# Scaling a gated layer's values by thirds, and moving the norms' second sums behind the next weight split

## The chip, the cores and the metric
The kernel runs on one core of one Trainium2 chip. The metric is the device time of one execution in microseconds (us), as the median of several runs. A profiled execution gives the trace from which every duration below is read. TensorE (PE), VectorE (DVE), ScalarE (ACT), GpSimd (POOL) and SyncE (SP) each run their own instruction stream and wait for each other on semaphores.

## What is computed
The input x has 512 positions of 1024 values. Three layers follow one another, each with a normalisation that is modulated from a conditioning vector c:

```
mod = silu(c) @ ada_w + ada_b                     # shifts, scales, gates
h   = rms_norm(x) * (1 + sc1) + sh1
y   = chunked_relpos_attention(h)                 # layer 0
y   = chunked_spatial_gating(h)                   # layer 1, the gated layer
x   = x + g1 * y
h   = rms_norm(x) * (1 + sc2) + sh2
x   = x + g2 * (relu(h @ w1)**2 @ w2)             # feed-forward of layers 0 and 1
x   = hybrid_layer(x)                             # layer 2: sparse attention and a state space part
```

The gated layer is

```
z    = gelu(h @ w_in);  u, v = split(z)           # 3072 columns each
v    = rms_norm(v)
vm   = W_s v + b_s                                # mixes positions inside windows of 128
y    = (u * vm) @ w_out
```

All arithmetic is 32-bit. A matrix product is computed as three products of a high and a low part.

## The kernel before
**Weights.** All weights pass through SBUF as 136 slabs of 128x2048 numbers. SyncE loads a slab into one of two raw buffers as soon as the slab two before it has been split. A slab is split in two steps: ScalarE copies it to its high part (`w_hi`, line 1050), VectorE subtracts to get the low part (`w_lo`, line 1480). There are two buffers for the parts too, so ScalarE's copy of a slab waits until TensorE is through with the slab two before (`slab_used`), and TensorE waits for `lo_done` before its first product with a slab. Line 474 holds the three products of every step.

**Order.** Nothing schedules the work: each engine's instructions stand in the order in which the code of its block issues them, and an instruction that waits holds back all that stand behind it on its engine. Results go to eight PSUM banks used in turn; `bank()` on TensorE waits (`acc_free`) until the bank used eight turns ago has been released.

**Tails and heads.** The last product of each of the first four blocks (attention out, feed-forward 0, gated layer out, feed-forward 1) is a `tail`, and what follows is a `head`. In a tail the last four of eight output tiles are computed in two halves of 256 positions: `half_tiles(x, 0)`, then `half_tiles(x, 1)`, over the same two slabs. While TensorE does the second half, ScalarE and VectorE already normalise the first. For each half the norm goes: ScalarE squares the tiles (`square`, line 1105), VectorE adds them up (`add_square`, line 1537), TensorE sums over the partitions with a vector of ones (`sums`, lines 533 and 534), ScalarE takes the root (`root`, line 1136), VectorE inverts it (`invert`, line 1584), TensorE spreads it (`spread`, line 543), and then `apply` on VectorE and `high_norm` on ScalarE make the high and low parts of h (lines 1597, 1149, 1606). The head's first products need h of the first half (`h_ready`) and its first slab; those with the second half of h come after two slabs' worth of half tiles. In `head` (before a feed-forward) the second half's `sums(1)` stands after the first half tile, `(j, m, k) == (0, 0, 7)`, and `spread(1)` six steps later, at `(0, 1, 5)`. In `head_natural` (before the gated and the hybrid layer) they stand after the first and the second tile of slab 0, and both result banks of a half are taken before its first product.

In what follows the two slabs of a head are called C and D, and the slab after them E. ScalarE splits C in the middle of `high_norm(0, split)`. It splits D in its `head()`, after the four squares of the second half. VectorE does its part of C in `apply(0, split)` and of D at the start of its `head()`, ahead of `invert(1)`. E is split at tile 6 of `ffn` (`if o == 6`), on ScalarE and VectorE.

**Modulation.** GpSimd loads the 128x1024 pieces of `ada` into two buffers in turn, and VectorE multiplies each with c and sums it (`ada`, line 1504). `ADA_FFN` says at which slabs of a quarter of a feed-forward VectorE takes one piece; the eight slots of a quarter are its four up slabs (0 to 3) and its four down slabs (4 to 7). Beside the slabs VectorE also does stages of tables for the state space part (`s5_stage`), and GpSimd stores these tables; the order of its loads and stores is derived from `ADA_FFN` too.

**Gated layer.** After the six panels of v, VectorE reduces the squares, inverts the root and scales v by position (line 2024: four instructions, one for each 128 positions, all 3072 columns). Then come three chunks of eight tiles of u: TensorE multiplies a tile of u (24 products), then mixes the same tile of v in `mix` (line 809); the first mix waits for `bv_scaled`.

```
for t in range(TT):
    ts_(b_v[:, t, :], b_v[:, t, :], rstd[:, t:t + 1], None, ALU.mult).then_inc(sem("bv_scaled"), 1)
for ch in range(CHUNKS):
    for s in range(4):
        split()
```

## Time and profile before
| | |
|---|---|
| median of 3 runs | 1845.28 us (1842.94 to 1848.31) |
| the profiled execution | 1844.67 us, of which the trace's span is 1842.5 us |
| TensorE busy | 1760.9 us, 96% of the span |
| VectorE busy | 1165.5 us, 63% |
| ScalarE busy | 667.8 us, 36% |
| GpSimd busy | 101.3 us, 5% |
| granted TensorE clock, mean | 0.99 |
| DMA | 245.98 MB, mean 134 GB/s |

The busy shares are averages over stages of different kinds, so what a change is worth is read at its place: in the timeline (what an engine did when, and in brackets how long it had been idle and who released it), in the table of waits (who waited for whom, in total), in the chain of waits (followed back from the end) and in the windows (busy time and granted clock in a stretch).

### The profile page before, as it was taken

How to read it: one execution, taken by the hardware profiler on the slowest of the kernel's cores; microseconds unless marked ns; L12 is line 12 of the kernel's file. 1: busy time of each engine (PE TensorE's matmuls, PEld its weight loads, DVE VectorE, ACT ScalarE, POOL GpSimd, SP SyncE). 2: the span in 40 equal slices, each digit the busy share in tenths (PEclk: the TensorE clock that was granted, in tenths of full speed). 3: DMA queues.
4: the chain of work that ended last, by engine and by line, in shares of the span. 5: the costliest groups of instructions: out<-in, count | busy, mean ns of one | idle time of the engine just before them, and what ended most of it. 6: DMA issues, size and time to landing. Idle time of an engine off the chain costs nothing.

```text
span 1842.5 us, 24232 instructions
## 1 busy us (share of the span) xinstructions
PE 1760.9 (96%) x9361; PEld 1465.6 (80%) x9361; DVE 1165.5 (63%) x2373; ACT 667.8 (36%) x1081; POOL 101.3 (5%) x194
## 2 busy tenths in 40 slices
PE   3998999999999999999999999999999998999999
PEld 2776768888888888878888898888888987777787
DVE  6777766876467656564454548874676579445574
ACT  3423673423232333233232335322323332366432
POOL 0001100001000100100000000010001100000000
PEclk9999999999999999999999999999999999999999
DMA  9354324335333534642323224354336222300351
GB/s 367 115 181 162 115 69 145 138 114 186 120 115 136 172 114 155 212 164 92 137 91 138 75 97 146 135 171 164 140 129 201 96 91 92 127 34 24 138 195 46
DMA packets 45470, 245.98 MB, mean 134 GB/s; under 512 B 6256, under 2 KB 6480, under 8 KB 27440
## 3 DMA queue, kind: packets, MB, share of 16 engines
q1 hardware_dynamic: 24848, 155.36, 23.3%
q0 software_dynamic: 20512, 89.11, 14.4%
q8 instruction: 74, 1.21, 0.3%
q14 instruction: 36, 0.29, 0.1%
HBM read 229.23 MB, written 15.22 MB: 133 GB/s over the span
## 4 chain that ended last, share of the span: by engine, by line
PE 81%; DVE 11%; ACT 3%; issue 2%; DMA 2%; SPq 0%; DVEq 0%; ACTq 0%
PE ps L474 70%; DVE w_lo L1480 2%; PE ps L935 2%; DMA ada_raw<-in_ada 1%; PE ps L809 1%; PE ps L916 1%; PE ps L925 1%; ACT w_hi L1050 1%; PE ps L644 1%; DVE ada_raw L1504 1%; PE ps L667 1%; PE ps L653 1%; DVE ada_first L1865 1%; DVE pre L1597 1%; PE ps L957 1%
## 5 line engine op out<-in xcount | busy, mean ns | idle before, releaser
L1480 DVE TENSOR_TENSOR w_lo<-w_raw,w_hi 128x2048 fp32r<-128x2048 f32 x136 | 311.6, 2291 | 153.8 <-ACT w_hi L1050 153.5
L1050 ACT ACTIVATE w_hi<-w_raw 128x2048 fp32r<-128x2048 f32 x136 | 260.0, 1912 | 361.7 <-PE ps L474 339.0
L474 PE MATMUL ps<-h_hi,w_hi 128*128 128x512 f32 (+1 forms) x1008 | 379.1, 376 | 9.9 <-DVE w_lo L1480 6.5
L474 PE MATMUL ps<-h_lo,w_hi 128*128 128x512 f32 (+1 forms) x1008 | 374.8, 372 | 0.0
L474 PE MATMUL ps<-h_hi,w_lo 128*128 128x512 f32 (+1 forms) x1008 | 374.5, 372 | 0.0
L474 PEld LDWEIGHTS ps<-h_hi,w_hi 128*128 128x128 f32 x1008 | 191.8, 190 | 43.7 <-DVE w_lo L1480 7.0
L474 PEld LDWEIGHTS ps<-h_hi,w_lo 128*128 128x128 f32 x1008 | 191.7, 190 | 32.6
L474 PEld LDWEIGHTS ps<-h_lo,w_hi 128*128 128x128 f32 x1008 | 191.8, 190 | 31.3
L474 PE MATMUL ps<-hid_hi,w_hi 128*128 128x512 f32 (+1 forms) x576 | 211.3, 367 | 0.0
L474 PE MATMUL ps<-hid_hi,w_lo 128*128 128x512 f32 (+1 forms) x576 | 210.6, 366 | 0.0
L474 PE MATMUL ps<-hid_lo,w_hi 128*128 128x512 f32 (+1 forms) x576 | 210.5, 366 | 0.0
L474 PE MATMUL ps<-w_hi,h_hi 128*128 128x512 f32 (+1 forms) x480 | 187.1, 390 | 17.4 <-DVE h_lo L1885 9.9
L474 PE MATMUL ps<-w_lo,h_hi 128*128 128x512 f32 (+1 forms) x480 | 184.2, 384 | 0.0
L474 PE MATMUL ps<-w_hi,h_lo 128*128 128x512 f32 (+1 forms) x480 | 183.8, 383 | 0.0
L1504 DVE CUSTOM_DVE_ANT_0 ada_raw<-ada_raw,cond 128x1024 f32<-128x1024 f32 x104 | 126.0, 1221 | 45.2 <-DMA ada_raw<-in_ada 44.1
L474 PEld LDWEIGHTS ps<-w_hi,h_hi 128*128 128x128 f32 x480 | 93.2, 194 | 38.3 <-issue 6.3
L474 PEld LDWEIGHTS ps<-hid_hi,w_hi 128*128 128x128 f32 x576 | 108.6, 189 | 17.7
L474 PEld LDWEIGHTS ps<-hid_lo,w_hi 128*128 128x128 f32 x576 | 108.6, 189 | 17.6
L474 PEld LDWEIGHTS ps<-hid_hi,w_lo 128*128 128x128 f32 x576 | 108.6, 189 | 17.3
L395 POOL DMA_DIRECT2D ada_raw<-in_ada x104 | 55.6, 535 | 1049.3 <-DVE mod_s L1504 985.2
L474 PEld LDWEIGHTS ps<-w_hi,h_lo 128*128 128x128 f32 x480 | 93.2, 194 | 17.1
L474 PEld LDWEIGHTS ps<-w_lo,h_hi 128*128 128x128 f32 x480 | 93.2, 194 | 16.5
(395 smaller groups left out, 2400.5 us busy)
## 6 DMA issues: line engine op xcount, KB each, us to landing
w_raw<-in_slabs SPq DMA_DIRECT2D x136, 1024.0 KB, 4.8
ada_raw<-in_ada POOLq DMA_DIRECT2D x104, 512.0 KB, 5.1
s_tables<-s_tab POOLq DMA_DIRECT2D x4, 2692.0 KB, 9.2
s_t<-s_tables POOLq DMA_DIRECT2D x4, 2692.0 KB, 9.8
ada_first<-in_ada SPq DMA_DIRECT2D x16, 512.0 KB, 15.1
a_bias<-in_a_bias POOLq DMA_DIRECT2D x16, 256.0 KB, 3.3
xT<-in_xT SPq DMA_DIRECT2D x4, 512.0 KB, 6.3
s_toeplitz<-KTp POOLq DMA_DIRECT2D x32, 64.0 KB, 3.3
```

The lines of the kernel that those rows point to most:

```text
L395: gp.dma_start(ada_raw[:, k % 2, :], I["ada"][k]).then_inc(sem(f"ada_in{k % 2}"), 16)
L474: last = mm(o, l, r, start=start and n == 0, stop=stop and n == 2)
L644: last = mm(ps[(s + j) % 3][:, 0:n], q, k, start=True, stop=True)
L653: last = nc.tensor.transpose(ps[3 + u % 2][:, j:j + P], a_p[:, u % 8, j:j + P], ident[:])
L667: last = mm(ps[5 + i % 2][HD * par:HD * par + HD, it * P:(it + 1) * P], value(UNITS_A[u + par], j), a_pt[:, (u + par) % 4, j * P:(j + 1) * ...
L809: last = mm(b[:, t * P:(t + 1) * P], b_v[:, t, gm * P:(gm + 1) * P], b_ws[:, gm // 3, :], start=True, stop=True)
L916: last = mm(ps[(s + g) % 3][:, 0:n], hqr[r, i, ts], hk[r, br - 1, 0:n], start=True, stop=True)
L925: last = nc.tensor.transpose(ps[3 + u % 2][:, j:j + P], h_p[:, u % 5, j:j + P], ident[:])
L935: last = mm(o, h_pt[:, u % 3, j * P:(j + 1) * P], hv[:, j, vc], start=j == 0, stop=j == it)
L1050: A(w_hi[s][:], w_raw[:, s, :], ACT.Copy).then_inc(sem("hi_done"), 1)
L1480: tt(w_lo[s][:], w_raw[:, s, :], w_hi[s][:].bitcast(F32), ALU.subtract).then_inc(sem("lo_done"), 1)
L1504: V.tensor_tensor_reduce(out=w, in0=w, in1=cond[:, which, :], scale=1.0, scalar=0.0, op0=ALU.mult, op1=ALU.add, accum_out=mod_s[:, o:o + 1 ...
```

## The change
Four things change. The values of the gated layer are scaled for the first 1024 columns only before the chunks, and each later third in four instructions, one after each split of the four u slabs of the chunk before (`scale_v`). `ADA_FFN` of layer 0 has slot 1 in place of slot 0. ScalarE splits D right behind `high_norm(0, split)`, ahead of the squares of the second half. TensorE does `sums(1)` and `spread(1)` later: in `head` at `(0, 1, 5)` and `(1, 0, 3)`, in `head_natural` after the second tile of slab 0 and after the first tile of slab 1; and there each bank is taken just before its first product.

```diff
--- before.py
+++ after.py
@@ -49,7 +49,7 @@
 ADA_FIRST = 16
 
 ADA_QKV = 16
-ADA_FFN = (4, (0, 2, 4, 5)), (6, (0, 1, 2, 3, 4, 5))
+ADA_FFN = (4, (1, 2, 4, 5)), (6, (0, 1, 2, 3, 4, 5))
 ADA_BV = 0, 4, 4, 5, 4, 4
 
 
@@ -588,9 +588,9 @@
             def head():
 
                 def beside(j, m, k):
-                    if (j, m, k) == (0, 0, KT - 1):
+                    if (j, m, k) == (0, 1, 5):
                         sums(1)
-                    if (j, m, k) == (0, 1, 5):
+                    if (j, m, k) == (1, 0, 3):
                         spread(1)
                 reserve(1)
                 half_tiles(H, 0, lambda k: h_ready(0, k), beside)
@@ -601,11 +601,13 @@
 
                 reserve(1)
                 for half in range(2):
-                    bs = [bank(), bank()]
+                    bs = []
                     for j in range(2):
                         s = (c.base("slab") + j) % 2
                         wait(pe, "lo_done", c("slab", 1 + j))
                         for t in range(2):
+                            if j == 0:
+                                bs.append(bank())
                             ts = slice(HT * half + t * P, HT * half + (t + 1) * P)
                             for kk in range(4):
                                 k, cols = 4 * j + kk, slice(kk * 512, (kk + 1) * 512)
@@ -616,11 +618,10 @@
                                 last.then_inc(sem("slab_used"), 1)
                             elif j:
                                 last.then_inc(sem("acc_full"), 1)
-                            if half == 0 and j == 0:
-                                if t == 0:
-                                    sums(1)
-                                if t == 1:
-                                    spread(1)
+                            if (half, j, t) == (0, 0, 1):
+                                sums(1)
+                            if (half, j, t) == (0, 1, 0):
+                                spread(1)
                 c.add("slab", 2)
                 c.add("norms")
 
@@ -802,8 +803,8 @@
                     def mix(m):
 
                         gm = KT * ch + 2 * s + m
-                        if gm == 0:
-                            pe.wait_ge(sem("bv_scaled"), TT)
+                        if gm % KT == 0:
+                            pe.wait_ge(sem("bv_scaled"), TT * (ch + 1))
                         b = bank()
                         for t in range(TT):
                             last = mm(b[:, t * P:(t + 1) * P], b_v[:, t, gm * P:(gm + 1) * P], b_ws[:, gm // 3, :], start=True, stop=True)
@@ -1123,6 +1124,7 @@
                     square(o, 0)
                 root(0)
                 high_norm(0, split)
+                split()
                 for o in range(4, KT):
                     c.add("bank")
                     c.add("slab" if o % 2 else "full")
@@ -1152,7 +1154,6 @@
 
             def head():
 
-                split()
                 root(1)
                 high_norm(1)
 
@@ -2020,11 +2021,18 @@
             V.tensor_reduce(stat[:, 0:TT], vss[:], AX.X, ALU.add).then_inc(sem("v_red"), 1)
             dve.wait_ge(sem("v_std"), 1)
             step(V.reciprocal(rstd[:, 0:TT], stat[:, 0:TT]))
+
+            def scale_v(t, ch):
+                v = b_v[:, t, KT * P * ch:KT * P * (ch + 1)]
+                ts_(v, v, rstd[:, t:t + 1], None, ALU.mult).then_inc(sem("bv_scaled"), 1)
+
             for t in range(TT):
-                ts_(b_v[:, t, :], b_v[:, t, :], rstd[:, t:t + 1], None, ALU.mult).then_inc(sem("bv_scaled"), 1)
+                scale_v(t, 0)
             for ch in range(CHUNKS):
                 for s in range(4):
                     split()
+                    if ch < CHUNKS - 1:
+                        scale_v(s, ch + 1)
                     for m in range(2):
                         gm = KT * ch + 2 * s + m
                         full(m)
```

**ScalarE at the end of a tail** (here the attention's; the four tails read alike). `w_hi` and `w_hi_54` are the two high buffers, C and D in this order; `pre`, `h_hi` belong to the norm, `sq_x`, `sq_84` are the squares, `stat` is the root. Before:

```order
L1149 ACTIVATE h_hi<-pre_87,mod 128x256 x4
L1050 ACTIVATE w_hi<-w_raw 128x2048
L1149 ACTIVATE h_hi<-pre_87,mod 128x256 x4
L1105 ACTIVATE sq_x<-xT 128x256 x3
L1105 ACTIVATE sq_84<-xT 128x256
L1050 ACTIVATE w_hi_54<-w_raw 128x2048
L1136 ACTIVATE stat<-ps,eps 128x2
```

and now:

```order
L1151 ACTIVATE h_hi<-pre_87,mod 128x256 x4
L1051 ACTIVATE w_hi<-w_raw 128x2048
L1151 ACTIVATE h_hi<-pre_87,mod 128x256 x4
L1051 ACTIVATE w_hi_54<-w_raw 128x2048
L1106 ACTIVATE sq_x<-xT 128x256 x3
L1106 ACTIVATE sq_84<-xT 128x256
L1138 ACTIVATE stat<-ps,eps 128x2
```

D's split moved from behind the four squares to ahead of them.

**VectorE at the start of the gated layer's chunks.** `b_v` are the values, `b_vm` the mixed tile, `g_lo` the low part of the product. Before:

```order
L2022 RECIPROCAL rstd<-stat 128x4
L2024 TENSOR_SCALAR b_v<-b_v,rstd 128x3072 x4
L1480 TENSOR_TENSOR w_lo_56<-w_raw,w_hi_54 128x2048
L2037 SCALAR_TENSOR_TENSOR b_vm<-ps,bv_g,b_bs 128x512
L2041 TENSOR_TENSOR b_vm<-b_vm,b_u 128x512
L2043 TENSOR_TENSOR g_lo<-b_vm,g_hi 128x512
L2037 SCALAR_TENSOR_TENSOR b_vm<-ps,bv_g,b_bs 128x512
L2041 TENSOR_TENSOR b_vm<-b_vm,b_u 128x512
```

and now:

```order
L2023 RECIPROCAL rstd<-stat 128x4
L2027 TENSOR_SCALAR b_v<-b_v,rstd 128x1024 x4
L1481 TENSOR_TENSOR w_lo_56<-w_raw,w_hi_54 128x2048
L2027 TENSOR_SCALAR b_v<-b_v,rstd 128x1024
L2045 SCALAR_TENSOR_TENSOR b_vm<-ps,bv_g,b_bs 128x512
L2049 TENSOR_TENSOR b_vm<-b_vm,b_u 128x512
L2051 TENSOR_TENSOR g_lo<-b_vm,g_hi 128x512
L2045 SCALAR_TENSOR_TENSOR b_vm<-ps,bv_g,b_bs 128x512
```

The four instructions became a third as wide, and one more of this width stands behind each split of the first two chunks.

**VectorE in the first quarter of the first feed-forward**, around tiles 4 and 5 and the split of E (`w_lo`); the two `ISA` rows are one piece of the modulation. Before:

```order
L1733 SCALAR_TENSOR_TENSOR s_t_176<-s_kk,s_th 128x8
L1734 SCALAR_TENSOR_TENSOR s_th<-s_kk,s_t_176 128x8
L1735 TENSOR_SCALAR s_th<-s_th 128x8
L1504 ISA ada_raw,mod_s<-ada_raw,cond 128x1024
L1504 ISA mod_s 128x1
L1666 SCALAR_TENSOR_TENSOR relu_94<-ps,relu 128x256
L1698 TENSOR_TENSOR hid_lo<-relu_94,hid_hi 128x256
L1666 SCALAR_TENSOR_TENSOR relu_94<-ps,relu 128x256
L1698 TENSOR_TENSOR hid_lo<-relu_94,hid_hi 128x256
L1480 TENSOR_TENSOR w_lo<-w_raw,w_hi 128x2048
```

and now:

```order
L1734 SCALAR_TENSOR_TENSOR s_t_176<-s_kk,s_th 128x8
L1735 SCALAR_TENSOR_TENSOR s_th<-s_kk,s_t_176 128x8
L1736 TENSOR_SCALAR s_th<-s_th 128x8
L1667 SCALAR_TENSOR_TENSOR relu_94<-ps,relu 128x256
L1699 TENSOR_TENSOR hid_lo<-relu_94,hid_hi 128x256
L1667 SCALAR_TENSOR_TENSOR relu_94<-ps,relu 128x256
L1699 TENSOR_TENSOR hid_lo<-relu_94,hid_hi 128x256
L1481 TENSOR_TENSOR w_lo<-w_raw,w_hi 128x2048
```

The piece that stood ahead of tile 4 (`relu_94`) now stands behind E's split and the table stage that follows it.

## Rows read from the trace of the kernel before

**Rows 1.** The page, part 1: busy time, share of the span, instructions, by engine.
```profile
PE 1760.9 (96%) x9361; PEld 1465.6 (80%) x9361; DVE 1165.5 (63%) x2373; ACT 667.8 (36%) x1081; POOL 101.3 (5%) x194
```

**Rows 2.** Waits of TensorE over the whole run: us in total, times, longest.
```profile
PE ps L809 <- DVE b_v L2024: 4.1, 1, 4.1
PE ps L533 <- ACT sq L1105: 4.0, 2, 2.0
PE ps L474 <- DVE pre L1597: 3.7, 2, 1.8
```

**Rows 3.** Timeline of VectorE where the values are scaled: start us, us, instruction, idle before.
```profile
820.46 7.01 DVE L2024 TENSOR_SCALAR b_v<-b_v,rstd 128x3072 f32<-128x3072 f32 x4
```

**Rows 4.** Chain of waits, same place: start us, us, what.
```profile
827.52 1.85 PE ps L809 x8
829.37 6.39 PE ps L474 x24
836.65 5.46 PE ps L474 x24
```

**Rows 5.** Windows: us, busy PE, PEld, DVE, ACT, POOL, granted clock, DMA, GB/s.
```profile
827.50:829.40 1.90, 1.88 (x9) 1.88 (x10) 1.90 (x1) 0.00 (x0) 0.00 (x0) 0.58 0.00 0
342.37:345.27 2.90, 0.01 (x2) 0.01 (x1) 2.35 (x2) 2.87 (x9) 0.00 (x0) 1.00 0.40 160
682.31:684.14 1.83, 0.00 (x1) 0.03 (x1) 1.83 (x6) 0.84 (x2) 1.53 (x3) 1.00 0.14 54
684.14:688.55 4.41, 4.41 (x13) 3.47 (x13) 3.48 (x10) 2.53 (x6) 0.55 (x2) 0.61 0.96 364
```

**Rows 6.** VectorE by form: a scaling 512 wide.
```profile
L1978 DVE TENSOR_SCALAR a_p<-a_p,row_inv 128x512 f32<-128x512 f32 x16 | 7.1, 484 | 0.3
```

**Rows 7.** Head of the first feed-forward, timelines of ScalarE, VectorE and TensorE.
```profile
315.31 0.51 ACT L1149 ACTIVATE h_hi<-pre,mod 128x256 fp32r<-128x256 f32 x1 [0.28 <-DVE pre L1597]
316.89 0.81 ACT L1105 ACTIVATE sq_x<-xT 128x256 f32<-128x256 f32 x2 [1.07 <-DVE xT L1542]
319.25 1.90 ACT L1050 ACTIVATE w_hi<-w_raw 128x2048 fp32r<-128x2048 f32 x1
...
318.81 0.41 DVE L1537 TENSOR_TENSOR acc<-acc,sq_x 128x256 f32<-128x256 f32 x1
321.25 2.29 DVE L1480 TENSOR_TENSOR w_lo<-w_raw,w_hi 128x2048 fp32r<-128x2048 f32 x1 [2.02 <-ACT w_hi L1050]
...
319.40 0.38 PE L533 MATMUL ps<-ones,acc 128*128 128x1 f32 x2 [1.98 <-ACT sq L1105]
...
323.67 0.71 PE L543 MATMUL ps<-ident,rstd 128*128 128x128 f32 x4 [0.97 <-DVE rstd L1584]
```

**Rows 8.** Chain of waits, between the first half's two norm products.
```profile
304.64 2.25 PE ps L474 x18
```

**Rows 9.** Same feed-forward, where its third slab is split: VectorE, then ScalarE.
```profile
337.45 0.17 DVE L1735 TENSOR_SCALAR s_th<-s_th 128x8 f32<-128x8 f32 x1
339.06 1.22 DVE L1504 CUSTOM_DVE_ANT_0 ada_raw<-ada_raw,cond 128x1024 f32<-128x1024 f32 x1 [1.44 <-DMA ada_raw<-in_ada]
...
340.99 1.90 ACT L1050 ACTIVATE w_hi<-w_raw 128x2048 fp32r<-128x2048 f32 x1
```

**Rows 10.** Head of the gated layer, timelines of VectorE, ScalarE and TensorE.
```profile
680.30 2.29 DVE L1480 TENSOR_TENSOR w_lo<-w_raw,w_hi 128x2048 fp32r<-128x2048 f32 x1 [0.41 <-ACT w_hi L1050]
...
683.30 0.47 DVE L1597 SCALAR_TENSOR_TENSOR pre<-xT,mod_a,ps 128x256 f32<-128x256 f32 x1
...
687.74 1.90 ACT L1050 ACTIVATE w_hi<-w_raw 128x2048 fp32r<-128x2048 f32 x1
...
692.21 0.60 PE L543 MATMUL ps<-ident,rstd 128*128 128x128 f32 x4
```

**Rows 11.** Second feed-forward, its third slab: VectorE's split, TensorE's first product.
```profile
1135.78 2.29 DVE L1480 TENSOR_TENSOR w_lo<-w_raw,w_hi 128x2048 fp32r<-128x2048 f32 x1 [1.07 <-ACT w_hi L1050]
...
1138.35 0.40 PE L474 MATMUL ps<-h_hi,w_hi 128*128 128x512 f32 x1
```

## The prediction

> **What bounds the kernel now.** I read the page first, then TensorE's waits, then the places where they stand. The page shows TensorE busy for 1760.9 of 1842.5 us [rows 1], so the most that any reordering can return is 81.6 us of idle time, and what an edit returns has to be found in a wait of TensorE that it shortens. In the table of waits the reader is to see three that the diff touches [rows 2]: one of 4.1 us for the scaled values, two of 2.0 us for the squares ahead of `sums(1)`, two of 1.8 us for the last `pre` of a first half. The chain of waits then shows what follows the first of them, and the windows show the granted clock behind such waits. All times below are those of one profiled execution of 1844.67 us (span 1842.5, 2.2 around it); the median of the runs is 0.6 above it. About 0.3%, or 5.5 us, is what a measurement can tell from no change here.
>
> **The scaling.** Four instructions of 3072 columns take 7.01 us from 820.46 [rows 3]. TensorE wanted the values 4.1 us before 827.52, at 823.4. Behind the wait it is slow as well: the mix and the next tile took 1.85 and 6.39 us where the later pair takes 0.89 (835.76 to 836.65) and 5.46 [rows 4]; the granted clock is 0.58 there, so most of that stretch ran at the lower of the two levels, 1.2 instead of 2.4 GHz [rows 5]. From 823.4 to 836.65 are 13.2 us; undisturbed the same work (mix, tile, mix) is 0.89 + 5.46 + 0.89 = 7.2. So the wait costs 6.0 us in all. Now: 512 columns take 0.48 us [rows 6], 3072 take 1.75, so 1024 take 0.48 + (1.75 - 0.48) / 5 = 0.74 and four of them 3.0: ready at 823.4, as TensorE comes. What is left of the wait lies between 0 and 0.2 us, and a wait of that size was followed by a low clock nowhere; I take 0. **Term: -6.0.** The other eight instructions (5.9 us of VectorE) go beside u slabs of 2 x 6.35 us on TensorE, in which no wait for VectorE stands now; nothing shows. If that cover went, each would cost 0.74. The mixes of the later thirds find their values ready over 20 us early.
>
> **The piece of modulation in the first feed-forward.** Ahead of E's split VectorE ends its table stage at 337.6, waits 1.44 us for a load, works on the piece, and only at 340.2 takes up tile 4; ScalarE's part of E follows at 340.99 [rows 9], and TensorE stands from 342.37 to 345.27 [rows 5]. Without the piece this chain is 340.2 - 337.6 = 2.6 us shorter and E can start at 342.7. **Term: -2.6**, if nothing earlier in the head moves VectorE. The piece itself (1.2 us, its load long landed) comes after the split, beside E's 48 products of 0.23 us, 10.9 in all [rows 4]. In later quarters it changes slots beside slabs of 11 us; GpSimd's load for slot 4 now stands behind the eight table stores, two slabs or 22 us before its use. Nothing for these.
>
> **The heads before the two feed-forwards.** ScalarE now does D's split at the end of the high parts, 315.8, to 317.7; the first square, at 316.89 before, comes 0.8 later [rows 7]. From it to `sums(1)` were 2.5 us, so the sums can go at 320.2. TensorE was there at 317.4 and waited 1.98; now it has 18 products more to do, which take 2.25 [rows 8], so it comes at 319.7 and waits 0.5. D's low part starts behind the last add (319.2 + 0.8 = 320.0) and is there at 322.3, where it was 323.5. The sums take 1.0 (319.40 to 322.70, where TensorE stood before the spread, less the 2.25), six products 0.7: TensorE is at D at 321.9, waits 0.5, does twelve more, 1.4, and spreads at 323.8, where it was 323.67. So the second half's norm comes no earlier, but TensorE stands 18 products further on: 2.1 us gained. Its steps with the second half's h then begin at about 328.6, at 0.36 each, while VectorE finishes them every 0.8 us until about 331; by this the last one is just in time (0 to 0.5 us lost). But E holds the gain back. In the first feed-forward TensorE comes to E at 340.3 and waits until 342.7, so the term above is all. In the second no slot moved: E's low part was there at 1138.07 and TensorE started at 1138.35 without waiting [rows 11]; now it comes at 1136.2 and waits about 2 us. **Term: -0.2**, between -0.4 and 0.
>
> **The heads before the gated and the hybrid layer.** TensorE was free at 682.31, C's low part there at 682.6, but the first tile started at 684.14 [rows 5, 10], since the second of its two banks is released by the last `pre`, which ends at 683.8. Now the first tile needs one bank less and starts at 682.8. Its two tiles end at 688.3. This head follows the first one at 368.5 us (D's split at 687.74 against 319.25 [rows 7, 10]), so its sums can go at 320.2 + 368.5 = 688.7, end at 689.7, and D is there at 690.9: a wait of 1.2. Half a slab, 2.73, then the spread, 0.6, and another 2.73: the second half starts at 696.9. Before it was 692.21 + 0.6 + 5.46 = 698.3. The low clock behind the 1.83 us wait cost nothing then, because the spread had to wait for D (687.74 + 1.90 + 2.29 = 691.9) and the inversion behind it anyway. **Term: 2 x -1.4 = -2.8.**
>
> **Sum** with the clock as it was: -6.0 - 2.6 - 0.2 - 2.8 = -11.6, 1833.1 us.
>
> **The clock.** A stretch at the low level costs 4.41 x (1 - 0.61) = 1.7 us [rows 5]. Behind waits of 1.83 us (two) and 2.90 us it came, behind the two of 2.0 it did not [rows 2, 7]: three of five. After the change three such places stand where nothing absorbs it: the wait for E in the second feed-forward (2.0 us, new), and in the two natural heads a row of 0.5, 0.4 and 1.2 us with the tiny products of the sums between. I count one and a half of three, the broken ones being the less likely: 2.6 us. So -11.6 + 2.6 = -9.0, 1835.7 on this execution and up to 1836.3 on the median; I forecast 1835.9.
>
> The Trainium skill (TensorE: Matmul & The Clock Gate, Part 1) puts the low level behind TensorE standing idle throughout; by that rule none of the three places would slow down, and the time would be 1833.1. The rows speak against it, since 1.83 us of idling was enough twice. The same section says that the monitor runs free, so that one kernel differs from run to run; no run here shows that yet.
>
> **Rivals.**
> - *No low clock at the three places.* What the page's rule would give. For it: the two 2.0 us waits, the broken waits. Against it: the 1.83 us ones. 1844.7 - 11.6 = 1833.1.
> - *Waits that only move.* All three places slow down, 5.1 us, and TensorE catches up with the second half's h in each head, up to 0.5 each: -11.6 + 5.1 + 0 to 2 = -6.5 to -4.5, 1838 to 1840. For it: VectorE's norm is no earlier than before while TensorE is. Against it: the steps' arithmetic above comes out just in time.
> - *D's split becomes the bound; slower.* On ScalarE the four squares now stand behind an instruction that waits for D's raw slab and for the end of the tail. If it waits x us beyond 315.8, the squares, the sums, D's low part and the spread are x late, and TensorE, which already waits at the sums and at D, loses x in each of four heads. From x = 2.3 the gain is gone, from 3.6 the kernel is over 0.3% slower; at x = 4 it is 1835.7 + 16 = 1852. For it: the order leaves no other work to ScalarE there. Against it: TensorE is through with the tail before ScalarE gets there (in the first head it began the first half tile, 24 products or 2.9 us, before 317.4, so by 314.5; in the gated one it was free at 682.31, where ScalarE will be ready at 315.8 + 368.5 = 684.3), and D's load is issued when the slab two before it is split.
> - *The change doesn't do what it says*: the thirds could be late, with a mix of a later chunk waiting. They are issued a whole chunk ahead, so I give it nothing of its own.
>
> **How the numbers follow.** Forecast, one or two places slow, 1834 to 1838: 0.54. No low clock: 0.20. Waits that only move: 0.21, a third of it still under 1839.7. Slower: 0.05. Faster by over 0.3% then is 0.54 + 0.20 + 0.07, about 0.80; within 0.3% 0.15; slower 0.05. The range goes from no low clock, less 0.7 for runs that scatter, to the far end of the second rival: 1832.4 to 1840.4.
>
> **What would show it.** In the changed kernel: the wait for `b_v` at line 809's mix gone or under 0.2 us, and no low clock in that chunk; the first feed-forward's wait for E still over 2 us but ending 2.6 earlier relative to C; a new wait of about 2 us for E in the second; both `pre` waits gone and a wait for D's low part of about 1.2 in the natural heads; the squares' wait at 0.5. Wrong would be: D's split on ScalarE waiting for a semaphore, waits for h in the second half's steps, the clock low behind each head, or VectorE late for a slab in the first two chunks.

## The result and the profile after

| | before | changed |
|---|---|---|
| median of the runs | 1845.28 us (1842.94 to 1849.24, 5 runs) | 1832.71 us (1830.98 to 1836.74, 5 runs) |
| the profiled execution, its span | 1844.67 us, 1842.5 us | 1832.71 us, 1830.5 us |
| TensorE busy | 1760.9 us | 1757.2 us |

The ratio of the two is 0.9927, with an interval from 0.9914 to 0.994: 0.7% faster, some 12.6 us by the medians and 12.0 us by the profiled executions. (The ratio is not the quotient of the two medians, which is 0.9932; 0.9927 stands for 13.5 us.) Forecast were 9.0 us on the profiled execution, and 1835.9 us in a range of 1832.4 to 1840.4. The median lies just inside the lower end of that range; the ratio applied to the median of before gives 1831.8, which is outside. The direction and the list of places came out; the gain is larger than forecast.

The page of the changed kernel, part 1, answers to [rows 1]:

```profile
PE 1757.2 (96%) x9361; PEld 1462.1 (80%) x9361; DVE 1166.0 (64%) x2381; ACT 666.9 (36%) x1081; POOL 101.2 (6%) x194
```

TensorE's busy time fell by 3.7 us though it does the same 9361 products. That part of the gain is the clock, since products at the low level count as busy for longer (the 12 products further down take 4.45 us at a granted clock of 0.62 and 2.87 at 1.00). The other 8.3 us of the span are waits that are gone. TensorE's waits, as in [rows 2]:

```profile
PE ps L474 <- DVE w_lo L1481: 14.1, 9, 3.6
...
PE ps L474 <- issue: 2.0, 4, 0.5
...
PE ps L533 <- ACT sq L1106: 1.0, 2, 0.6
```

The waits for `b_v` (4.1) and for `pre` (3.7) are in the table no more, and the one for the squares fell from 4.0 to 1.0 us. The spreads' waits for `rstd` in the two feed-forwards, one of them in [rows 7], are gone too. In their place the waits for a low part grew. These are the two rows of before:

```profile
PE ps L474 <- DVE w_lo L1480: 10.2, 4, 3.6
...
PE ps L543 <- DVE rstd L1584: 2.3, 2, 1.3
```

Gone are 4.1 + 3.7 + 3.0 + 2.3 = 13.1 us. What came are 3.9 us for low parts and two starts of a head at which TensorE waits 0.5 us on its own issue, where before it waited for `pre`: 4.9 us, 8.2 net, close to the 8.3 above. The rows of the table that the change doesn't touch moved too, one by as much as 1.5 us, but they nearly cancel (0.3 us less together).

**The scaling.** Timeline of VectorE at the start of the gated layer's chunks, against [rows 3]:

```profile
814.91 2.74 DVE L2027 TENSOR_SCALAR b_v<-b_v,rstd 128x1024 f32<-128x1024 f32 x4
817.57 2.28 DVE L1481 TENSOR_TENSOR w_lo<-w_raw,w_hi 128x2048 fp32r<-128x2048 f32 x1
819.77 0.75 DVE L2027 TENSOR_SCALAR b_v<-b_v,rstd 128x1024 f32<-128x1024 f32 x1
820.43 0.74 DVE L2045 SCALAR_TENSOR_TENSOR b_vm<-ps,bv_g,b_bs 128x512 f32<-128x512 f32 x1
```

Four scalings 1024 wide take 2.74 us where the forecast had 3.0. They end at 817.65, and the first mix begins at 817.70. TensorE is busy for the whole 15 us around it, at the high level:

```profile
817.70 1.16 PE L810 MATMUL ps<-b_ws,b_v 128*128 128x128 f32 x8
```

```profile
811.00:826.00 15.00, 15.00 (x76) 12.53 (x75) 9.72 (x17) 7.10 (x8) 0.00 (x0) 1.00 0.22 77
```

The last scaling of the second third ends at 857.69, and the first mix that needs it starts at 912.10, so no later chunk is near a wait.

**The head of the first feed-forward**, TensorE, against [rows 7]:

```profile
314.62 0.36 PE L474 MATMUL ps<-h_hi,w_hi 128*128 128x256 f32 x1 [0.50 <-issue]
...
320.32 0.38 PE L533 MATMUL ps<-ones,acc 128*128 128x1 f32 x2 [0.45 <-ACT sq L1106]
...
322.40 0.38 PE L474 MATMUL ps<-h_hi,w_hi 128*128 128x256 f32 x1 [0.21 <-DVE w_lo L1481]
...
323.93 0.60 PE L543 MATMUL ps<-ident,rstd 128*128 128x128 f32 x4
...
342.79 0.50 PE L474 MATMUL ps<-h_hi,w_hi 128*128 128x512 f32 x1 [2.41 <-DVE w_lo L1481]
```

The forecast had the sums at 320.2, D at 322.4 (wait 0.5), the spread at 323.8 and E at 342.7. (This kernel reaches the tail 0.3 us later, at 303.99 against 303.69; counted from there, all four came 0.2 to 0.3 us earlier than forecast.) ScalarE in the same place:

```profile
315.62 0.51 ACT L1151 ACTIVATE h_hi<-pre,mod 128x256 fp32r<-128x256 f32 x1 [0.27 <-DVE pre L1598]
316.04 1.90 ACT L1051 ACTIVATE w_hi<-w_raw 128x2048 fp32r<-128x2048 f32 x1
```

D's split follows the last high part at once and waits for nothing.

**The head of the gated layer**, TensorE, against [rows 5, 10]:

```profile
678.71 0.47 PE L474 MATMUL ps<-w_hi,h_hi 128*128 128x512 f32 x1 [0.50 <-issue]
...
684.42 0.38 PE L533 MATMUL ps<-ones,acc 128*128 128x1 f32 x2
...
686.50 0.50 PE L474 MATMUL ps<-w_hi,h_hi 128*128 128x512 f32 x1 [1.03 <-DVE w_lo L1481]
...
689.37 0.61 PE L543 MATMUL ps<-ident,rstd 128*128 128x128 f32 x4
```

The head starts 0.50 us after the tail, no longer 1.83, and the wait for D's low part is 1.03 us. To compare the two kernels, count from the tail's first-half sums (672.19 before, 668.08 now): the second half's products began at 25.94 and begin at 24.49, 1.45 us earlier.

**The second feed-forward, and the head of the hybrid layer**, TensorE:

```profile
1126.54 0.50 PE L474 MATMUL ps<-h_hi,w_hi 128*128 128x512 f32 x1 [1.78 <-DVE w_lo L1481]
```

```profile
1470.26 0.50 PE L474 MATMUL ps<-w_hi,h_hi 128*128 128x512 f32 x1 [1.03 <-DVE w_lo L1481]
...
1474.71 0.60 PE L543 MATMUL ps<-ident,rstd 128*128 128x128 f32 x4
```

There is the new wait for E, 1.78 us where 2.0 was forecast. In the hybrid head the stretch from D to the spread takes 4.45 us, in the gated head 2.87 for the same 12 products. The windows give the reason (the granted clock is the third number from the end):

```profile
342.79:346.79 4.00, 4.00 (x18) 3.31 (x19) 3.66 (x24) 0.86 (x4) 0.53 (x1) 1.00 0.71 248
686.50:689.37 2.87, 2.87 (x12) 2.36 (x13) 0.03 (x1) 0.00 (x0) 0.00 (x0) 1.00 1.01 373
1126.54:1130.54 4.00, 4.00 (x18) 3.31 (x19) 3.67 (x24) 0.87 (x4) 0.53 (x1) 1.00 0.68 248
1470.26:1474.71 4.45, 4.45 (x13) 3.51 (x13) 0.02 (x1) 0.00 (x0) 0.00 (x0) 0.62 0.65 236
```

Of four places where TensorE starts again behind a wait, one is at the low level. In the kernel before, the stretch behind the wait for E was low too. This is its window (not among the rows above):

```profile
345.27:349.27 4.00, 4.00 (x12) 3.20 (x13) 3.10 (x23) 2.02 (x4) 0.00 (x0) 0.66 0.71 242
```

**Where the 12 us came from.** The program falls into five pieces, cut at the first-half sums of the four tails (line 533; before at 303.69, 672.19, 1099.47 and 1463.54, now at 303.99, 668.08, 1088.03 and 1451.84):

| piece | before | now | gain | of it |
|---|---|---|---|---|
| up to tail 1 | 303.69 | 303.99 | -0.3 | nothing of the change |
| first feed-forward | 368.50 | 364.09 | 4.4 | E 2.8 earlier; 1.6 clock behind E |
| gated layer | 427.28 | 419.95 | 7.3 | head 1.45; scaling 5.9 |
| second feed-forward | 364.07 | 363.81 | 0.3 | E as good as kept its place |
| hybrid layer | 378.96 | 378.66 | 0.3 | head 1.45, less 1.6 clock; 0.4 unexplained |

### The profile page after: what moved, and what is told of

Read it like the earlier page. It is cut to its first block, busy times and chain, and to the rows that moved or that the text cites. A ratio compares the mean times of both kernels' runs of the same rounds, so it can differ in the third digit from the quotient of the medians.

```text
span 1830.5 us, 24238 instructions
## 1 busy us (share of the span) xinstructions
PE 1757.2 (96%) x9361; PEld 1462.1 (80%) x9361; DVE 1166.0 (64%) x2381; ACT 666.9 (36%) x1081; POOL 101.2 (6%) x194
## 4 chain that ended last, share of the span: by engine, by line
PE 80%; DVE 12%; ACT 4%; issue 2%; DMA 2%; SPq 0%; DVEq 0%; ACTq 0%
PE ps L474 69%; DVE w_lo L1481 3%; PE ps L936 2%; PE ps L810 1%; DMA ada_raw<-in_ada 1%; PE ps L917 1%; ACT w_hi L1051 1%; DVE ada_raw L1505 1%; PE ps L926 1%; DVE ada_first L1866 1%; PE ps L645 1%; DVE pre L1598 1%; PE ps L654 1%; PE ps L668 1%; PE ps L958 1%
```

## The experiments

The theory under test is the forecast's own. Each edit returns the wait of TensorE that it takes away, unless something else is late at the same place; and behind each wait that is left, a low clock may or may not follow. Its rivals are that a wait only moves to the next engine that is late, that the clock and not the waits made the gain, and that one edit alone carries it. Each expectation, quoted as it was written, states what its theories give. All ratios are against the kernel before, run beside it on the same chip (medians 1846.52, 1846.14 and 1846.24 us in three groups of runs).

### The parts one at a time

**The thirds alone.**

```diff
-    ts_(b_v[:, t, :], b_v[:, t, :], rstd[:, t:t + 1], None, ALU.mult).then_inc(sem("bv_scaled"), 1)
+    scale_v(t, 0)
...
+        if ch < CHUNKS - 1:
+            scale_v(s, ch + 1)
```

> The kernel before with the scaling by thirds alone. Theory A (the terms add, each at its own place): the wait of 4.1 us for the values and the low clock behind it go, 5.9 us off, ratio 0.9968. Rival B (the low clock is a matter of chance and comes elsewhere): only the wait itself goes, 4.1 us, ratio 0.9978, and a low stretch stands in the gated chunks as before. Both: no wait of a chunk's mix for b_v, the four heads with the waits of before (2.0 at the sums, 1.8 before the natural heads, 2.9 for E).

Measured: 1837.74 us, ratio 0.9967 [0.995, 0.9984]. The gated piece took 421.40 us (672.87 to 1094.27), against 427.28: 5.88 us, the whole term. The waits in the heads stood as before, the 2.93 us one for E among them, but for one: the squares before the hybrid layer, for which TensorE now waits 0.76 us.

**Slot 1 in place of slot 0 alone.**

```diff
-ADA_FFN = (4, (0, 2, 4, 5)), (6, (0, 1, 2, 3, 4, 5))
+ADA_FFN = (4, (1, 2, 4, 5)), (6, (0, 1, 2, 3, 4, 5))
```

> The kernel before with slot 1 for slot 0 in layer 0 alone. Theory A: E of the first feed-forward starts 2.6 us earlier while TensorE comes to it as before (342.37), so the wait falls from 2.9 to 0.3 and the low clock behind it goes too: 2.6 + 1.7 = 4.3 us off, ratio 0.9977. Rival B (the waiting in the head decides, not the slot): under 1 us off, a wait for E of over 2 us left. Both: nothing at the other three heads.

Measured: 1841.43 us, ratio 0.9984 [0.9968, 1.0]. TensorE at E, in the kernel with the slot alone:

```profile
341.73 0.50 PE L474 MATMUL ps<-h_hi,w_hi 128*128 128x512 f32 x1 [0.25 <-DVE w_lo L1480]
```

The wait shrank from 2.90 to 0.25 us, and the piece of the program took 364.23 us, against 368.50: 2.65 us of wait and 1.6 of clock, since here the wait of 0.25 us was not followed by a low level. The profiled execution, 1849.69 us in all, had a long stretch of low clock in the hybrid layer, which the change doesn't touch; the total of this trace says nothing, its first piece does.

**Everything in the heads alone** (sums, spreads, D's split, banks; the scaling and the slot as before).

```diff
+                split()                       # ScalarE, behind high_norm(0, split)
-                    if (j, m, k) == (0, 0, KT - 1):
+                    if (j, m, k) == (0, 1, 5):
                         sums(1)
...
-                    bs = [bank(), bank()]
+                    bs = []
```

> The kernel before with D's split moved, the sums and spreads later and the banks taken one by one, without thirds and slot. Theory A: E of the first feed-forward still starts at about 345.2 with a wait of over 4.5 us (the gain there moves into the wait), 0.2 off in the second feed-forward, 1.4 in each natural head less 1.7 for each low clock: 1 to 3 us off, ratio 0.9984 to 0.9995. Rival C (the heads are what made the change better than forecast): 5 us or more off, ratio under 0.9973.

Measured: 1844.43 us, ratio 0.9991 [0.9982, 1.0001]. In the first feed-forward the head passes TensorE on earlier and E takes all of it back:

```profile
346.04 0.57 PE L474 MATMUL ps<-h_hi,w_hi 128*128 128x512 f32 x1 [4.62 <-DVE w_lo L1481]
```

4.62 us of wait for E, where 2.90 stood, and the low level behind it. This is the forecast's sentence "E holds the gain back", shown. (E itself starts 42.54 us behind the tail's sums, 41.58 before: in this trace a low level at 322.44 to 325.85, behind waits of 0.43 and 0.21 us in the head, came before it; without one, in the run of sums and split below, E starts at 41.44.) In the gated head D's products took 2.86 us, in the hybrid one 4.44:

```profile
691.38:694.24 2.86, 2.86 (x12) 2.36 (x13) 0.02 (x1) 0.00 (x0) 0.00 (x0) 1.00 1.01 375
1482.23:1486.67 4.44, 4.44 (x13) 3.49 (x14) 0.02 (x1) 0.00 (x0) 0.00 (x0) 0.62 0.69 236
```

**The banks alone.**

```diff
-                    bs = [bank(), bank()]
+                    bs = []
...
+                            if j == 0:
+                                bs.append(bank())
```

> The kernel before with the banks of the natural heads taken one by one, nothing else. Theory A: the first tile starts 1.4 us earlier, but the sums then wait for the squares (about 2.4 us) and the spread for D as before: 0 us off, ratio 0.9995 to 1.0005, with a wait at line 533 in place of the one for pre. Rival D (the bank alone gives the 1.5 us of each natural head): 3 us off, ratio 0.9984.

Measured: 1848.31 us, ratio 1.0014 [1.0005, 1.0023], slower by a little. The head of the gated layer, TensorE:

```profile
681.38 0.47 PE L474 MATMUL ps<-w_hi,h_hi 128*128 128x512 f32 x1 [0.50 <-issue]
...
686.47 0.38 PE L533 MATMUL ps<-ones,acc 128*128 128x1 f32 x2 [2.08 <-ACT sq L1107]
...
690.67 0.71 PE L543 MATMUL ps<-ident,rstd 128*128 128x128 f32 x4 [0.30 <-DVE rstd L1586]
```

The head begins 1.3 us earlier and the sums then wait 2.08 us for the squares: the wait moved. I hadn't expected a loss. The gated piece is as long as before (427.09 against 427.28 us). In the hybrid head the spread comes 21.04 us behind the tail's sums, 20.02 before: the stretch of low clock now lies behind the sums, close ahead of the spread, where nothing is left to absorb it. In the gated head of this trace the clock stayed high, and the spread comes at 19.91. That is 1.0 us in one head of one trace; the rest of the 2.6 us that the ratio says is not placed.

### The parts taken out one at a time

**The changed kernel again**, for its scatter.

> The changed kernel once more. Theory A (low clocks fall by chance at waits of about 2 us, each costing up to 1.7 us): the waits stand where they stood in the changed kernel, to 0.1 us (0.5 and 0.2 in the first head, 2.4 for E, 1.0 for D in the natural heads, 1.8 for E in the second feed-forward), but the low stretches stand at other places; ratio 0.992 to 0.995. Rival B (which wait slows the clock is fixed by the kernel): a low stretch at the hybrid layer's head alone, as in the changed kernel's trace.

Measured: 1834.05 us (1833.28 to 1834.14, 5 runs), ratio 0.9937 [0.9924, 0.9951]. Its waits in the heads and for E are those of the first trace, to 0.03 us. The clock is not. This is the window behind E:

```profile
341.27:345.27 4.00, 4.00 (x12) 3.21 (x13) 3.66 (x24) 0.87 (x4) 0.53 (x1) 0.64 0.67 231
```

The same wait of 2.41 us was followed by 0.64 here and by 1.00 in the trace above. The first feed-forward took 365.45 us, against 364.09.

**Without the thirds.** The edit is the first diff of this section, undone on the changed kernel.

> The changed kernel with all 3072 columns scaled at once, as before the change. Theory A: the wait of 4.1 us at the first mix and its low clock are back, 5.9 us more than the changed kernel, so heads, banks and slot together give 5 to 7 us, ratio 0.996 to 0.9975, which is more than slot alone (0.9984) and heads alone (0.9991) and near their sum (0.9975). Rival E (the parts multiply each other): under 0.995.

Measured: 1838.99 us, ratio 0.9963 [0.9951, 0.9975]. The wait of 4.11 us for `b_v` is back, and so is the low level behind it:

```profile
824.25:826.15 1.90, 1.90 (x9) 1.90 (x10) 1.90 (x1) 0.00 (x0) 0.00 (x0) 0.56 0.00 0
```

**Sums and split without the banks**, and nothing else of the change. The diff is against the kernel with everything in the heads.

```diff
-                    bs = []
+                    bs = [bank(), bank()]
...
-                            if j == 0:
-                                bs.append(bank())
```

> The kernel before with D's split and the sums moved, but both banks of a natural head taken at once as before. Theory A: the first tile of a natural head starts behind a wait of 1.8 us as before, then no wait for the sums, D ready: if the clock falls behind that wait the second half starts as late as before (0 us off in that head), if not 1.3 us off; so this is 0 to 3 us slower than with the banks (0.9991), ratio 0.9990 to 1.0005. Rival F (the banks give nothing in this company either): the same ratio as with them, 0.9991.

Measured: 1844.03 us, ratio 0.9993 [0.9984, 1.0002], against 0.9991 with the banks. The two waits of 1.83 us for `pre` are back at the start of the natural heads. The gated head, TensorE:

```profile
683.56 0.47 PE L474 MATMUL ps<-w_hi,h_hi 128*128 128x512 f32 x1 [1.83 <-DVE pre L1596]
...
689.11 0.28 PE L533 MATMUL ps<-ones,acc 128*128 128x1 f32 x2
...
692.88 0.61 PE L543 MATMUL ps<-ident,rstd 128*128 128x128 f32 x4
```

The head starts 1.3 us later than with the banks and then waits for nothing, neither squares nor D. Its spread stands 21.27 us behind the tail's sums; in the changed kernel it is 21.29. D's low part ends at 689.97 and TensorE takes it up at 690.02, 18.41 us behind the tail's sums; in the changed kernel, after its wait of 1.03 us, it is 18.42. So it is D's low part that sets the spread, and where TensorE spends its wait ahead of that, before C or before D, is all one. The banks are worth nothing measurable (the gated piece took 425.82 us, and 425.80 with them), and the 1.45 us of this head belong to the sums and the split.

**The sums and spreads where they were**, the rest of the change in (the edit in `head`; the one in `head_natural` is alike).

```diff
-                    if (j, m, k) == (0, 1, 5):
+                    if (j, m, k) == (0, 0, KT - 1):
                         sums(1)
-                    if (j, m, k) == (1, 0, 3):
+                    if (j, m, k) == (0, 1, 5):
                         spread(1)
```

> The changed kernel with sums(1) and spread(1) where they were before. Theory A: the squares come 0.8 us later and the sums are asked for at the old place, so TensorE waits 2.8 us in the two heads of feed-forwards and some 3.2 us in the natural heads, where its spread then also waits or nearly does; 1.5 us lost in each natural head and a low clock more likely there: 4 to 8 us slower than the changed kernel, ratio 0.995 to 0.9975. Rival G (the place of the sums does not matter since D's low part sets the pace): within 1.5 us of the changed kernel, ratio 0.9925 to 0.9940.

Measured: 1840.07 us, ratio 0.9966 [0.9954, 0.9979]. ScalarE's split ahead of the squares makes them late, and TensorE, which has not been given other work, stands for it in all four heads, 2.60 to 2.74 us. The gated one, and the clock behind it, which was low in all four heads:

```profile
685.47 0.59 PE L533 MATMUL ps<-ones,acc 128*128 128x1 f32 x2 [2.71 <-ACT sq L1107]
```

```profile
685.47:689.47 4.00, 4.00 (x13) 3.52 (x14) 2.20 (x2) 0.26 (x1) 0.00 (x0) 0.50 1.02 357
```

**D's split where it was**, the rest of the change in.

```diff
-                high_norm(0, split)
-                split()
+                high_norm(0, split)
...
             def head():
+                split()
                 root(1)
```

> The changed kernel with ScalarE splitting D behind the squares, as before. Theory A (D's low part sets the pace of the head): no wait for the squares, but D's low part comes 1.2 us later, TensorE waits for it about 2 us before the feed-forwards and 2.3 before the gated and hybrid layer, and each head ends 1.1 to 1.3 us later: 4.8 us slower than the changed kernel, a low clock more likely, ratio 0.996 to 0.998. Rival H (moving the sums alone does the work, D's split is free): ratio 0.9925 to 0.9940, the same as the changed kernel.

Measured: 1842.51 us, ratio 0.9987 [0.9974, 1.0]. The sums no longer wait, but D's low part is late and TensorE stands at D in all four heads. The gated one:

```profile
690.35 0.50 PE L474 MATMUL ps<-w_hi,h_hi 128*128 128x512 f32 x1 [2.74 <-DVE w_lo L1481]
```

In the first head the spread starts 22.63 us behind the tail's sums, 19.94 in the changed kernel, and E 41.55, against 38.80. So 2.7 us of lateness in the head go on to E and take the slot's term with them. Of these, 1.5 us are D itself (its first product is at 19.91 us, against 18.42); the rest is the clock, which was low in this head from 323.02 to 326.43, and in the other three too. The expectation had 4.8 us of loss against the changed kernel and a ratio of 0.996 to 0.998; the medians say 8.5 to 9.8 us, the four pieces behind the first tail 9.1. D was 1.3 to 1.5 us late where 1.1 to 1.3 was expected, and the low level, which came in every head, had been called "more likely" and given no price. The sums without the split lose, and the split without the sums loses; the two moves are one edit.

### Beyond the change

**The same slot move in the second feed-forward**, on top of the change. There too a piece of modulation stands ahead of E's split, and E's wait of 1.78 us is new.

```diff
-ADA_FFN = (4, (1, 2, 4, 5)), (6, (0, 1, 2, 3, 4, 5))
+ADA_FFN = (4, (1, 2, 4, 5)), (6, (1, 2, 3, 4, 5, 6))
```

> The changed kernel with layer 1's pieces at slots 1 to 6 instead of 0 to 5. Theory A (E's wait in the second feed-forward is VectorE's chain ahead of its split): the piece of 1.2 us leaves that chain, the wait of 1.8 us falls to 0.6, 1.2 us off the changed kernel and no low clock behind it. Rival B (the chain there is bound by ScalarE or by the release of C): the wait stays at 1.8, nothing changes. Ratio to the kernel before 0.992 to 0.9935.

Measured: 1830.81 us (1828.63 to 1834.30, 4 runs), ratio 0.9909 [0.9895, 0.9923].

```profile
1128.14 0.50 PE L474 MATMUL ps<-h_hi,w_hi 128*128 128x512 f32 x1 [0.67 <-DVE w_lo L1481]
```

E starts 37.39 us behind the tail's sums, 38.51 in the changed kernel, and the piece of the program takes 362.70 us, against 363.81: 1.1 us gained, all of it at E. It has the lowest median of all kernels here. It is faster than the kernel before, and by more than was expected (0.992 to 0.9935). Against the changed kernel its interval overlaps that one's first, 0.9914 to 0.994, and just misses its second, 0.9924 to 0.9951; what speaks for the edit is the 1.1 us of the trace, which is the size that the theory gave.

**Two more pieces of modulation behind E's split** in the first feed-forward.

```diff
                             if o == 4:
...
-                                if layer == 0:
-                                    ada(2, 0)
-                                    ada_put()
                                 beside(0)
                             if o == 6:
                                 split()
+                                if layer == 0:
+                                    ada(2, 0)
+                                    ada_put()
```

> The changed kernel with the two pieces and the put that stand ahead of tile 4 in the first feed-forward moved behind E's split. Theory A: VectorE's chain to E is 2.5 us shorter, the wait of 2.4 us for E becomes 0 to 0.2, 2.3 us off the changed kernel and no low clock at this place in any run. Rival B (the two pieces only use time that VectorE has): the wait stays over 2 us. Ratio to the kernel before 0.991 to 0.993.

Measured: 1836.95 us (1832.38 to 1847.04, 8 runs), ratio 0.995 [0.9934, 0.9967]. The medians are 2.9 and 4.2 us above those of the changed kernel's two groups, but the interval overlaps both of theirs. The gain that the theory forecast did not come. E's wait did shrink, to 0.46 us, but against the changed kernel E is only 0.4 us earlier (38.37 us behind the tail's sums, against 38.80), and TensorE arrives 1.5 us later. That lateness is not the edit's: in this trace, and in the next one, a low level stood in the head, behind the waits of 0.43 and 0.21 us:

```profile
322.42:326.42 4.00, 4.00 (x23) 4.00 (x22) 0.93 (x3) 0.41 (x1) 0.00 (x0) 0.57 0.73 264
```

The kernel without the thirds has the same code here, without this edit, and its trace has the same low stretch: there E came at 39.91, behind a wait of 2.00 us. So at a like clock the edit makes E 1.5 us earlier. That is less than the 2.5 us expected of the chain, in part because VectorE now waits 0.79 us there for ScalarE's share of the table stage. What it costs comes one slab later, as TensorE and VectorE tell (F is the slab after E):

```profile
341.95 0.50 PE L474 MATMUL ps<-h_hi,w_hi 128*128 128x512 f32 x1 [0.46 <-DVE w_lo L1481]
...
355.12 0.50 PE L474 MATMUL ps<-h_hi,w_hi 128*128 128x512 f32 x1 [1.99 <-DVE w_lo L1481]
```

```profile
341.81 1.22 DVE L1505 CUSTOM_DVE_ANT_0 ada_raw<-ada_raw,cond 128x1024 f32<-128x1024 f32 x1
...
342.96 1.22 DVE L1505 CUSTOM_DVE_ANT_0 ada_raw<-ada_raw,cond 128x1024 f32<-128x1024 f32 x1
...
348.92 1.23 DVE L1505 CUSTOM_DVE_ANT_0 ada_raw<-ada_raw,cond 128x1024 f32<-128x1024 f32 x1 [2.59 <-DMA ada_raw<-in_ada]
...
352.78 2.29 DVE L1481 TENSOR_TENSOR w_lo<-w_raw,w_hi 128x2048 fp32r<-128x2048 f32 x1 [1.06 <-ACT w_hi L1051]
```

```profile
343.33 0.55 POOL L395 DMA_DIRECT2D ada_raw<-in_ada  x1 [28.30 <-DVE mod_s L1505]
```

Three pieces now stand in a row with two buffers between them. GpSimd can issue the third load only when the first piece is done, at 343.33, and VectorE, which may not pass it by, waits 2.59 us until 348.92. Behind it stand the next tile and F's split. F comes 1.99 us late, where no wait was, and a low clock follows. The piece of the program took 367.60 us, against 364.09 and 365.45 in the two traces of the changed kernel.

**Both together.**

> The changed kernel with both: layer 1's slots 1 to 6 and the two pieces of the first feed-forward behind E's split. Theory A: the two gains add, 3.5 us off the changed kernel and up to 1 us more for low clocks that no longer come: ratio 0.9905 to 0.9925. Rival B: within 1 us of the changed kernel, 0.993.

Measured: 1833.19 us, ratio 0.9926 [0.9914, 0.9938]. The first feed-forward took 367.72 us as in the kernel above, the second 362.72 as in the one before it. Its wait at F is 1.91 us. Gain and loss add up place by place; the 3.5 us that the expectation added up did not come, and the ratio is that of the changed kernel.

### The clock behind equal waits

All traces together hold the same wait many times over, so it can be counted how often a low level followed. The wait of 1.03 us for D in the natural heads stands in seven traces of the kernels with both moves and the banks, 14 times. The 12 products behind it took 2.85 to 2.87 us in 5 of them, at a granted clock of 1.00, and 4.1 to 4.45 us in 9, at 0.62 to 0.68. Two such heads of one execution, the gated and the hybrid one, come out differently:

```profile
689.72:694.15 4.43, 4.43 (x13) 3.47 (x13) 0.02 (x1) 0.00 (x0) 0.00 (x0) 0.62 1.00 372
1473.97:1476.82 2.85, 2.85 (x12) 2.36 (x13) 0.02 (x1) 0.00 (x0) 0.00 (x0) 1.00 0.59 187
```

| place | wait | followed by the low level |
|---|---|---|
| the mix's wait for `b_v` (scaling in one) | 4.1 us | 6 of 6 |
| E, first feed-forward, slot as before | 2.9 to 5.1 us | 5 of 5 |
| E, first feed-forward, slot moved | 2.0 to 2.4 us | 2 of 5 |
| E, second feed-forward, sums and split moved | 1.6 to 1.8 us | 2 of 6 |
| D in a natural head | 1.03 us | 9 of 14 |
| first product of a natural head, banks as before | 1.8 us | 5 of 8 |
| squares, sums as before | 2.0 to 2.1 us | 5 of 10 |
| F, with the two pieces late | 1.9 to 2.0 us | 2 of 2 |
| squares, with the split moved and the sums not | 2.6 to 2.7 us | 4 of 4 |
| D, with the sums moved and the split not | 2.3 to 2.7 us | 4 of 4 |
| squares and D in a row, head of a feed-forward, both moved | 0.4 to 0.6 and 0.2 to 0.4 us | 6 of 16 |

Each costs 1.6 us where nothing absorbs it (4.45 against 2.87 us). The last row is one that neither the forecast nor the experiments reckoned with: two waits that together are 0.6 to 1.0 us. Where it happened in the second feed-forward the piece took 365.05 and 365.09 us, against 363.81 with no low level, so 1.2 to 1.3 us; in the first, E came 1.1 us later (39.91 against 38.80) for the same code.

## Why the prediction was off

**The scaling, -6.0.** Right: 5.9 us in the gated piece, with the thirds alone and in the change, and the wait and its low clock return when they are undone. The other eight scalings cost nothing that a trace shows, as forecast.

**The slot, -2.6.** Right as a shift: E starts 2.8 us earlier in its piece, and with the slot alone TensorE waits 0.25 us instead of 2.90.

**The heads of the feed-forwards, -0.2.** Right: counted from the tail, sums, D, spread and E came within 0.3 us of the forecast times in the first, the new wait for E is in the second, and the gain is 0.3 us. The heads' edits alone push E's wait to 4.62 us.

**The natural heads, 2 x -1.4.** Right in size: 1.45 us in the gated one. The hybrid one is the same without the low clock: in the two traces where it stayed high there (both with the two pieces late) the spread came 21.27 us behind the tail's sums, as in the gated head (21.29). The forecast started this head's chain with the bank that comes free earlier; by the run without banks that step carries none of it. D's low part does, as the chain's next step said. The wait of 0.4 us for the squares that was forecast here did not come, and the one for D was 1.03 us, not 1.2.

So the four terms, forecast at 11.6 us, measure 5.9 + 2.8 + 0.3 + 2.9 = 11.9 us.

**The clock, +2.6: the step that failed.** The prediction looked for low stretches at "three such places" that are new after the change and added the price of one and a half. It gave no term to the low level behind E in the first feed-forward, which stood in the trace of before: by its sum this level was there on both sides. In the profiled pair one of the three new places was low (hybrid head, +1.6), and the old one was not any more (-1.6): net 0 where +2.6 was forecast. 11.9 us is then the whole difference, 12.0 measured. That one place was left out matters more than the count, for the counts agree with the forecast's: 9 of 14 twice and 2 of 6 are 1.6 places of three. Taken over all traces, the old place fell from 5 of 5 to 2 of 5, which is 1.0 us of gain that the sum lacked: -11.9 + 2.6 - 1.0 = -10.3 us. So of the 3 us between forecast and profiled pair about 1 is the omitted place, 0.3 the four terms, and the rest is how the clock fell in this pair. The feed-forward heads, which the forecast also put at nothing on both sides, had a low level in 4 of 8 before and in 6 of 16 after, at 0.2 to 2.0 and 1.0 to 1.3 us each; no net effect can be read from so few.

**What stays open.** For the two groups of runs of the changed kernel the medians say 12.6 and 12.1 us, the ratios 13.5 and 11.6. The 1.3 to 3.2 us between these and the 10.3 us are of the size of the intervals (some 2.4 us to each side), and clocks in parts of the program that the change doesn't touch differ from trace to trace as well. Whether the change makes those rarer too, or the scatter made them so, no run here separates.

**The rivals.** *No low clock at the three places* gave 1833.1, nearest to the result, but that is luck: by its reason it was wrong, since the low level does follow 1.03 us waits, and one of the three places was low in the profiled execution. The rule of the Trainium skill on which it was built (TensorE: Matmul & The Clock Gate, Part 1: the low level comes after TensorE has stood idle throughout) does not fit the rows: in the natural heads TensorE stood for 0.50 us, worked for 6.8 us, stood for 1.03 us, and the granted clock of the next 12 products was 0.62 to 0.68 in 9 of 14 cases. The other sentence of that section, that the monitor runs free and a kernel differs from run to run, is borne out by the same 2.41 us wait at 0.64 and at 1.00. *Waits that only move* came true in part: for the banks alone and for each of the two moves alone, not for all together. *D's split as the bound* did not come: the split started at once behind the last high part. With the sums left in place it is the bound, at 2.6 to 2.7 us a head, and even then the kernel was faster than before.

## What to carry to other kernels

Moving a wait pays only when every engine that meets there moves with it: sums moved without the split, the split without the sums, and the banks without both each left TensorE standing 2 to 2.7 us at the next place, while sums and split together gained 1.45 us a head. In a strict order, ask of each instruction put behind another what it waits for: a piece of work whose buffer comes free only by its neighbour in the same row holds up the whole engine. And where short waits bring a slower clock at random, count such places on both sides of a change, the ones it removes as well as the ones it adds, and compare a trace of an experiment only with one in which the clock fell the same way.

## What the hardware showed

That waits of 1.03 us, right behind the tiny products of the sums, are followed by the low level in 9 of 14 cases is more than I had expected, and waits of 0.4 and 0.2 us in a row still in 6 of 16. One and the same wait goes either way between executions of one kernel (2.41 us: 1.00 and 0.64). The scaling of 1024 columns, which no row of before had, took 0.75 us alone and 2.74 in a row of four; the forecast had 0.74 and 3.0.
